# Cross attention: three values products placed earlier in TensorE's order, behind the next unit's scores

## The reference, cut to what matters

```python
def mem_cross_attn(hn, mem, wq, wkv, wo):          # hn 512 x 1024, mem 256 x 1024, 4 heads of 128
    q = (hn @ wq).reshape(b, s, CA_HEADS, CA_HEAD_DIM)
    kv = (mem @ wkv).reshape(b, mem.shape[1], 2, CA_HEADS, CA_HEAD_DIM)
    sc = jnp.einsum('bshd,bmhd->bhsm', q, kv[:, :, 0]) * CA_HEAD_DIM ** -0.5
    p = jax.nn.softmax(sc, axis=-1)
    o = jnp.einsum('bhsm,bmhd->bshd', p, kv[:, :, 1]).reshape(b, s, CA_WIDTH)
    return o @ wo
```

## Time and profile before

| what | value |
|---|---|
| median of 3 runs | 1809.7 us (1809.41 to 1812.27) |
| profiled execution: span from first to last instruction | 1807.3 us |
| TensorE (PE) busy | 1662.9 us, 92% |
| VectorE (DVE) busy | 593.9 us, 33% |
| ScalarE (ACT) busy | 476.2 us, 26% |
| GpSimd (POOL) busy | 251.8 us, 14% |
| DMA | 484.29 MB, 268 GB/s over the span |

### The profile page before, as it was taken

One profiled execution on the slowest core, in us unless ns is written; L12 is line 12 of the kernel. 1 busy time (PEld: TensorE's weight loads), 2 busy tenths in 40 slices (PEclk: granted clock), 3 DMA queues, 4 the chain that ended last, 5 costly groups with the idle time before them and its releaser, 6 DMA issues.

```text
span 1807.3 us, 21401 instructions
## 1 busy us (share of the span) xinstructions
PE 1662.9 (92%) x8783; PEld 981.5 (54%) x8783; DVE 593.9 (33%) x1068; ACT 476.2 (26%) x880; POOL 251.8 (14%) x118
## 2 busy tenths in 40 slices
PE   7999999989899898898988989889899999999998
PEld 5897686653343432434324334243286558878886
DVE  4987784540210201202002020020176462260074
ACT  4366725310000100001001000010155433353242
POOL 0004511000000000000000000000050574106430
PEclk9999999999999999999999999999999999999999
DMA  9444055359999999999999999999920104203121
GB/s 341 136 131 129 1 163 221 145 207 429 428 428 428 429 428 428 428 428 428 429 429 428 429 429 428 428 429 429 415 78 0 48 5 124 94 15 107 62 110 47
DMA packets 65601, 484.29 MB, mean 268 GB/s; under 512 B 10268, under 2 KB 17909, under 8 KB 39807
## 3 DMA queue, kind: packets, MB, share of 16 engines
q1 hardware_dynamic: 65535, 483.36, 65.8%
HBM read 480.94 MB, written 2.41 MB: 267 GB/s over the span
## 4 chain that ended last, share of the span: by engine, by line
PE 76%; DMA 15%; DVE 4%; issue 2%; ACT 2%; POOL 1%; POOLq 0%; DVEq 0%; SPq 0%; ACTq 0%
PE psum L553 22%; PE psum L1943 19%; DMA ring<-in_expert_w_down 13%; PE psum L1963 8%; PE psum L1925 4%; PE psum L1972 3%; PE psum L1581 2%; PE psum L2912 2%; PE psum L705 2%; PE psum L2588 2%; PE psum L683 2%; PE psum L670 2%; DMA ring<-in_expert_w_gu 1%; PE psum L2603 1%; PE psum L1714 1%
## 5 line engine op out<-in xcount | busy, mean ns | idle before, releaser
L1943 PE MATMUL psum<-ring,work_area 128*64 128x512 f32 x2032 | 444.9, 594 | 32.2 <-DMA ring<-in_expert_w_gu 24.5
L1943 PEld LDWEIGHTS psum<-ring,work_area 128*64 128x64 f32 x2032 | 146.7, 137 | 323.7 <-issue 276.1
L1963 PE MATMUL psum<-ring,work_area 128*64 128x512 f32 x1024 | 231.2, 606 | 16.2 <-DMA ring<-in_expert_w_down 14.8
L2042 DVE TENSOR_TENSOR work_area<-psum,work_area 128x512 f32<-128x512 f32 x32 | 20.6, 686 | 589.1 <-ACT work_area L2004 589.1
L1963 PEld LDWEIGHTS psum<-ring,work_area 128*64 128x64 f32 x1024 | 73.3, 139 | 163.1 <-issue 141.2
L2004 ACT ACTIVATE work_area<-psum 128x512 f32<-128x512 f32 x32 | 17.4, 594 | 482.0 <-PE psum L1943 482.0
L2198 POOL TENSOR_TENSOR hn<-x_res,ring 128x1024 f32<-128x1024 f32 x3 | 9.0, 3013 | 887.7 <-DVE x_res L2049 887.7
L2107 POOL TENSOR_TENSOR block_lo<-ring,part_hi 128x1024 fp32r<-128x1024 f32 x35 | 86.3, 2474 | 139.6 <-ACT part_hi L2100 139.2
L2049 DVE TENSOR_TENSOR x_res<-psum,x_res 128x512 f32<-128x512 f32 x64 | 44.3, 692 | 155.5 <-PE psum L1972 155.5
L553 PE MATMUL psum<-h_hi,part_hi 128*128 128x512 f32 x240 | 93.7, 391 | 1.0 <-DVE hn L826 1.0
L553 PE MATMUL psum<-h_hi,block_lo 128*128 128x512 f32 x240 | 93.4, 389 | 0.0
(11 more groups left out here) (520 smaller groups left out, 2746.0 us busy)
## 6 DMA issues: line engine op xcount, KB each, us to landing
ring<-in_expert_w_gu SPq DMA_DIRECT2D x127, 2048.0 KB, 27.1
ring<-in_expert_w_down SPq DMA_DIRECT2D x64, 2048.0 KB, 21.2
ring<-in_w_in SPq DMA_DIRECT2D x12, 2048.0 KB, 8.6
extra<-in_w_mod SPq DMA_DIRECT2D x4, 1536.0 KB, 10.5
ring<-in_w_out SPq DMA_DIRECT2D x3, 2048.0 KB, 12.6
ring<-in_ca_wkv SPq DMA_DIRECT2D x2, 2048.0 KB, 12.9
hn<-in_w_mod SPq DMA_DIRECT2D x2, 1536.0 KB, 6.8
x_res<-in_x SPq DMA_DIRECT2D x2, 1024.0 KB, 13.3
```

What stands on the lines that cost most here:

```text
L1943: ins = pe.matmul(psum[h * 64:(h + 1) * 64, c, :], xsT[:, k, e * CAP:(e + 1) * CAP], w[:, (2 * c + h) * BANK:(2 * c + h + 1) * BANK], star ...
L1963: ins = pe.matmul(psum[n * 64:(n + 1) * 64, 6, :], hidT[b][:, j, h, :], w[:, j, n * BANK:(n + 1) * BANK], start=(q == 0 and j == 0), stop= ...
```

## The change

The plan gets a parameter for how many turns later the O comes, and a function that moves each O behind the n-th scores that follow it. TensorE and VectorE get lists of their own; ScalarE keeps the plan's list. Only the cross attention's call uses the new parameters: `o_later=1`, O behind one more S on TensorE, behind two more S on VectorE.

```diff
-        def plan_attention(heads, step):
+        def plan_attention(heads, step, o_later=O_LATER):
...
-                while (n_out + 1) * T + O_LATER <= turned or (turned == n and n_out < n // T):
+                while (n_out + 1) * T + o_later <= turned or (turned == n and n_out < n // T):
...
+        def values_behind(order, n):
+            moved = list(order)
+            for v in [item for item in order if item[0] == "O"]:
+                at = moved.index(v)
+                scores = [i for i in range(at, len(moved)) if moved[i][0] == "S"][:n]
+                if scores:
+                    moved.insert(scores[-1], moved.pop(at))
+            return moved
...
-                      turned_from=None, besides={}, outs=None, before_last_out=None):
+                      turned_from=None, besides={}, outs=None, before_last_out=None, o_later=O_LATER, o_behind=(0, 0)):
...
-            nj, units, order = plan_attention(heads, step)
+            nj, units, order = plan_attention(heads, step, o_later)
+            pe_order, dve_order = (values_behind(order, n) for n in o_behind)
...
-                for kind, i in order:
+                for kind, i in pe_order:
...
-                for kind, i in order:
+                for kind, i in dve_order:
...
-            lambda i, q, o: split_o(i, o), late=False, turners=(act,), before_last_out=lambda: ca_out_pe(0, (0, 1)))
+            lambda i, q, o: split_o(i, o), late=False, turners=(act,), before_last_out=lambda: ca_out_pe(0, (0, 1)),
+            o_later=1, o_behind=(1, 2))
```

## The result

The changed kernel takes 1811.1 us (median of 20 runs, 1808.43 to 1813.93) against 1809.19 us of the kernel before (20 runs). The ratio is 1.0015, 95% interval 1.0009 to 1.0020, that is 2.7 us more (1.6 to 3.6). The forecast was 1811.0 us and +1.3 us. The time is met, and the shift was taken too small.

The account below looks back on a forecast made before the run. The prediction took cross attention to be on the critical path, VectorE pacing its middle plus a wait for TensorE. It summed +0.80 + 0.79 - 0.29 = +1.30 us onto 1809.7, giving 1811.0 us, range 1808.8 to 1813.4.

Parts of the forecast that it names:

- What bounds the stage, and what the change does: Cross attention: VectorE sets the mid-stage pace plus a 0.67 us wait; only three values products move on TensorE.
- O0: First head's values product on TensorE: starts at 316.16, 0.65 us earlier, delaying unit 9's scores; costs 0.80 us.
- O1 and O2: Second and third heads' values products: start at 322.20 and 328.24, 0.79 us more lost, then 0.29 back at the tail.
- The release from ScalarE to TensorE: Delay from the end of ScalarE's copy to the values product: 0.06 us, at most 0.3, three times over +0.7.
- the order's cost: Cross attention: the new TensorE order makes the last values product 1.30 us late, shift +0.5 to +2.3.
- The clock: TensorE in cross attention: waits of about 1.6 and 1.9 us cost no clock loss, being behind dense work.
- rival D: TensorE's clock falls to 1.2 GHz at two cross-attention waits, 1.7 us each: 4.7 us slower, 1814.4; chance 0.10.
- The Trainium skill's rule: Short idling between matmul groups cycling through PSUM banks makes TensorE's clock oscillate; would give 1811.0 plus 3.4 us.
- Behind the stage: Projection to expert weight stream: everything shifts alike, first release 401.0 to 402.3, so 1.30 us go through in full.
- rival C: Expert stream or router loads bind earlier than TensorE, so the shift is absorbed: 1809.7; chance 0.15.
- Rival B: Cross attention: VectorE's waits for the first two values products (0.67 each) vanish, nothing replacing them: 1808.4; chance 0.12.
- The number: Whole kernel: 1811.0 us, +1.3 us on the median of 1809.7; this forecast's chance 0.63.

Follow-up runs that it names:

- e7: Changed kernel with each of ScalarE's copies of a turn put ahead of the exponential in front of it; stage length 20.28 us, ratio to before 0.9993.
- e1: Kernel before, run again without edit; stage length 21.28 us, ratio to before 0.9998.
- e11: Kernel before with ScalarE's copies put ahead of its exponentials; stage length 21.29 us, ratio to before 1.0002.
- e6: Changed kernel with the first two values products behind one more scores each (units 9 and 13); stage length 20.45 us, ratio to before 0.9994.
- e3: Changed kernel with only the third head's values product moved up, the first two placed as before; stage length 21.16 us, ratio to before 0.9997.
- e4: Changed kernel with four added score products filling the wait ahead of the third values product; stage length 23.07 us, ratio to before 1.0006.
- e10: Changed kernel with only the first two values products moved and three score products added before unit 13's turn; stage length 23.19 us, ratio to before 1.0015.
- e2: Changed kernel, run again without edit; stage length 24.74 us, ratio to before 1.0016.
- e9: Changed kernel with three added score products filling the wait ahead of the second values product only; stage length 24.75 us, ratio to before 1.0013.
- e5: Changed kernel with only the first two values products moved up, the third in its old place; stage length 24.81 us, ratio to before 1.0019.
- e12: Changed kernel with values products behind two scores and ScalarE's copies ahead of exponentials, second measurement; stage length 19.30 us, ratio to before 0.9989.

## Why the prediction was right, and where it was not

**What bounds the stage, and what the change does: right.** Same instructions, the same stream on VectorE; 21401 instructions in both.

**O0: right.** Forecast 316.16 against an entry of 309.41, that is 6.75 us in; measured 6.83. The wait for S9 replaced that for O0 (1.62 us measured, 1.5 forecast). e7 shows the cause, the copy of T3 behind an exponential.

**O1 and O2: right in kind, small in size.** Forecast 12.79 and 18.83, measured 13.04 and 19.24. Two terms were mis-sized. The release from ScalarE to TensorE was taken at 0.06 us; it is 0.15 (copy from 319.66, 0.37 long, O1 at 320.18). And an O that has waited holds the queue for 1.79 us (313.97 to 315.76), not 1.72. Three times 0.09 and three times 0.07 make 0.48 us, and the order's cost of 1.78 us is 1.30 + 0.48. The text named the release as an unknown, with a bound of +0.7, and the order's cost came out inside its +0.5 to +2.3; the 0.07 was in none of its terms. (From those terms the bounds would be 1.3 + 0.7 = +2.0 and 1.3 - 0.6 = +0.7; the wider ones have no term of their own.)

**The clock: wrong.** "I take no loss, being behind dense work" is the step that failed. The clock fell behind the wait of 2.07 us, at a price of 1.66 us, just under the 1.7 of one fall in rival D, which had 0.10 with two falls. The forecast took the longest harmless wait (1.00 us) and the shortest known with a fall (2.51 us), and put waits of 1.6 and 1.9 us on the harmless side. That was a choice between two rows, not something they showed. They came out at 1.64 and 2.07 us, and only behind the second did the clock fall. The Trainium skill's rule that was weighed ("TensorE: Matmul & The Clock Gate", section "A second HAM failure mode: psum-queue depth-cycling", idling between groups of matmuls makes the clock oscillate) is borne out in part: the trace of the changed kernel agrees with it so far as there is one fall to 0.50 and one return, behind a single long wait. With waits of up to 1.00 us between the groups (before, e1, e11) the clock stayed at 1.00, and the two falls, 3.4 us, that the prediction put beside the rule were not seen.

**Behind the stage: right.** From O3 to the first expert product it is 66.5 us before (330.70 to 397.19) and 66.4 after (331.87 to 398.25): the shift goes through, and rival C falls. From O3 to the end of the span it is 1476.6 us in both. Rival B, the early product pays, does not hold for this change; but its condition (S9 out in time) is what e6 meets, in another order, and there the gain is 0.84 us.

**The number.** 1811.0 lies 0.1 from the measured 1811.1. That is partly luck: the order was taken 0.48 us and the clock 1.66 us too low, while the median of before moved from 1809.7 to 1809.19 with more runs and the two medians came out only 1.9 us apart. Against before, the shift forecast was 1.3 us, and 2.7 us (1.6 to 3.6) was measured.

## What to carry to other kernels

Before moving a product up in an in-order queue, ask two things: which instruction of another engine releases it, and what stands in front of that instruction on its own engine (here an exponential in front of a copy); and what is queued behind the product. The same early place, with the next scores behind it both times, lost 3.44 us (1.66 of them the clock's), and gained 1.01 us once the releasing copy came first; with two scores in front of the product it gained as well. A wait of two microseconds on TensorE costs more than itself if the clock falls behind it, so fill it or keep it short, and look at the granted clock in windows of 1 us.

## What the runs showed of the hardware that was not expected

- Waits of 1.50 us (e3), 1.28 us (e6) and 0.89 us (e7) in this stage left the clock at 1.00, and so did 1.64 us in front of O1 where the later wait was filled (e4, e10). It fell behind 2.07 us in front of O2 in the changed kernel, e2 and e9, and behind waits of 1.64, 1.57 and 0.35 us along the stage in e5. Whether e5 would hold without its wait of 1.64 us was not tried. Each time it was back at 1.00 before O3. In the changed kernel, e2 and e9 the lengths were equal within 0.02 us although their entries differed by up to 2.8 us.
- The same happens ahead of the first expert, behind a wait of 2.50 us in every run: the 64 gather products take 7.38 us where the clock held (e7, e11, e12), 8.96 or 9.01 in nine executions, those of before and after among them, and 10.33 in e4 and 10.31 in e10. That alone spreads executions by up to 2.95 us, and in e4's profiled execution it took back 1.3 (10.33 - 9.01) of the 1.66 us that the filled wait had won. TensorE's timelines of e4 and of e12 at that place:

```profile
386.73 10.33 PE L1941 MATMUL psum<-work_area,hn 128*128 128x128 f32 x64 [2.51 <-DVE work_area L2039]
```

```profile
385.20 7.38 PE L1946 MATMUL psum<-work_area,hn 128*128 128x128 f32 x64 [2.50 <-DVE work_area L2044]
```

Why it falls in one execution and not in another there was not tried. The two longest are the two kernels with the late wait filled; whether that is chance is open.
